# Index queries for fewer token tiles, modulation sums on TensorE and later keys in a hybrid attention, retention and expert block

## The chip, the cores and the metric

The kernel runs on one core of a Trainium2 chip. The metric is the device time of one execution in microseconds (us); the median over several executions is compared. Engines are named as in the profile: PE is TensorE, DVE is VectorE, ACT is ScalarE, POOL is GpSimd, and SP is the engine that mostly issues DMAs. PEld is TensorE loading a stationary operand.

## The reference, cut to what matters

One transformer-like layer over 1024 tokens of width 1024. Only the beginning matters for the change:

```
mod = c @ w_ada + b_ada;  sh1, sc1, gt1, sh2, sc2, gt2 = split(mod, 6)      # 6 x 1024
h   = rmsnorm(x, g) * (1 + sc1) + sh1                                       # 1024 tokens x 1024
qa, ka, va, qi, ki, wi, qb, kb, vb, gb = split(h @ w_in)                     # 4688 columns
# sparse attention, by blocks of 128 queries; qi has 16 index heads of 64, ki one, wi 16 weights
score = sum_h wi[h] * relu(qi[h] . ki / 8)      # causal by chunks of 64 keys
sel   = top_k(score, 256)                       # softmax attention over the selected keys only
```

Then come retention on the second group of heads, the output projection, a mixture of 32 experts (top 2 in one group of 8) and a last norm. A query of token tiles 0 and 1 (tokens 0 to 255) sees at most 256 keys, so its top 256 are all of them; its scores decide nothing.

## The kernel before, in words

Tokens are worked in 8 tiles of 128. There are 5 instruction streams, ordered by hand, with semaphores between them. The part that the change touches runs up to the first score.

**Loads (SP, L467 to L488).** SP issues in order: the whole table of constants (`cst`, 1190 columns), four small vectors, the 8 tiles of x, the 80 columns of w_in for key and index weights (`w_keys`), the columns sc1 and then sh1 of w_ada (4 MB each, in five DMAs, L481), and the first 512 columns of w_in (`load_weights(0)`, L475). After the transposes of x it issues the second 512 columns, and when both index chunks are projected (`a_proj` at `FIRST[RETAIN]`) the third.

**Norm and turn.** ACT squares x (L752), POOL takes the root (L645), DVE scales the tiles (L1045), PE transposes them (L1658), ACT copies the result to `hT` (L764).

**Modulation sums.** DVE multiplies w_ada by c row block by row block and adds (L1054, L1056: 16 instructions of 128x1024, each waited for). This leaves 128 partial sums for each column. PE adds them over the partitions with 8 products against a column of ones for each of the two parts (L1672), which also puts the result in columns. DVE adds the bias (L1060 to L1064) and applies scale and shift to `hT` (L1069, 16 instructions of 128x512; the first half of the tokens first).

**Keys.** PE computes 80 columns (64 of the index key, 16 weights) in plain fp32, over all tokens (L1708, 16 matmuls), ahead of any projection. ACT copies them out (L809, L813), PE turns them (L1716), DVE rotates them (L1135 to L1144), PE turns them again (L1722), and DVE writes `kiD` (L1147).

**Projections in three passes.** Every other projection splits both operands in a rounded high part and a rest: ACT makes the high part (`split_high` L783, `hidden_high` L790), DVE the low part (`split_low` L1118, `hidden_low` L1127), and PE adds high x high, high x low and low x high (`split_product`, L1651 to L1653). A unit is one tile of tokens by one chunk of columns: `project(u)`, 8 steps of 3 matmuls of 128x512. The index queries are chunks 0 and 1, with 8 units each. For each unit ACT copies the result (L805), DVE rotates 8 heads (L1080 to L1086), PE turns the tile (`a_turn`, L1684), and DVE writes `qiT` (L1100). `a_copy` of the first three units waits for the turned keys (`key_pe` at 5).

**Beside it.** ACT issues 8 DMAs that clear `y_dram` (L772, 3 MB each), one after every second copied unit. POOL loads the later modulation columns in 8 steps of 2 MB (L651): the first when 8 units are projected, each further one when PE has used the one before (`late_used`, L1737). `late_products` holds the PE stream while it waits for its load.

**Scores.** For tiles 2 to 7 and 16 heads, 96 units: PE (L1752), relu on ACT (L830), weighted sum on DVE (L1167, L1169). One step of `late_products` stands after every 12 units, the first after 7. PE starts the scores when all turned units are in `qiT`.

The rest (retention projections, top-k by bisection, attention, experts) is not edited but for numbering: units are looked up in a list `UNIT` where `divmod(u, T)` stood.

Of the kernel before, what the change touches and what calls it, by code (L numbers as in the profile page):

```python
# [6 lines left out]
F32 = mybir.dt.float32  # L7
# [9 lines left out]
P = 128  # L17
# [41 lines left out]
FIRST_SCORED = TOPK // P  # L59
SCORED = range(FIRST_SCORED, T)  # L60
# [6 lines left out]
def constant_table():  # L67
# [4 lines left out]
    parts["before"] = (p[:, None] < p[None, :])  # L72
    parts["causal"] = (p[None, :] >= p[:, None])
# [3 lines left out]
    lg = np.log1p(-np.exp2(-5.0 - np.arange(HB)))  # L77
    parts["kfac"] = np.exp(-(p[:, None] + 1.0) * lg[None]) * HD ** -0.5
# [42 lines left out]
def block_kernel(nc, x, ccol, pos, w_ada, b_cols, b_gt1, b_sc2, b_sh2, b_gt2, g_cols, g_ffn, g_final, w_in, w_o, w_router,  # L121
                 w_up, w_gate, w_down, const, out):
    ctx = ExitStack()
    with ctx:
# [22 lines left out]
        def sb_before(name, shape):  # L147
# [16 lines left out]
        ada_slot = [BIG[:, 8192:16384].rearrange("p (k c) -> p k c", k=KD),  # L164
                    BIG[:, 16384:24576].rearrange("p (k c) -> p k c", k=KD)]
# [67 lines left out]
        W0 = work([("sq", (D,)), ("mac", (2, D)), ("ang", (T, 40)), ("k", (T, 40)), ("r", (T, 40)), ("c", (T, 40))])  # L233
        WA = work([("tmp", (3, 512)), ("s1", (128,)), ("s2", (128,)), ("trq", (2, 512)), ("R", (3, 1024))])
        w_keys = WK[:, 4352:4992].rearrange("p (k c) -> p k c", k=KD)
        keys_turned = WK[:, 0:1024]
        keys = WK[:, 1024:1664].rearrange("p (t c) -> p t c", t=T)
        key_rows = WK[:, 1664:2688].rearrange("p (t c) -> p t c", t=T)
        key_s1, key_s2 = [WK[:, a:a + 128].rearrange("p (t a d) -> p t a d", t=T, a=2) for a in (2688, 4992)]
# [89 lines left out]
        UNITS = len(CHUNKS) * T  # L329
        FIRST = {c: c * T for c in (INDEX, RETAIN, ATTEND)}  # L330
        turned = [u for u in range(UNITS) if CHUNKS[u // T][0] not in ("qb", "kb", "vb", "gb", "va")]
        NTURN = len(turned)
        TURN1 = RETAIN * T
        copied = [u for u in range(UNITS) if not RETAIN * T <= u < ATTEND * T]
        NCOPY = len(copied)

        def evacuated(u):

            c, t = divmod(u, T)
# [22 lines left out]

        ADA_PARTS = (((0, 4),), ((4, 8),), ((0, 4),), ((4, 6), (6, 8)))

        def ada_landed(part, a):

            return G("ada_last") if a == 6 else G(f"slot{part}")
# [97 lines left out]
        def _(sp):  # L465

            for dst, src in ((cst[:, :], const), (cc[:, :], ccol), (bc[:, :, :], b_cols), (gc[:, :], g_cols),  # L467
                             (posi[:, :], pos)):
                sp.dma_start(dst, src).then_inc(G("ld_const"), 16)
# [23 lines left out]
            for n in range(RETAIN, ATTEND):  # L493
                if n > RETAIN:
                    sp.wait_ge(G("a_proj"), T * n)
# [13 lines left out]
            sp.wait_ge(G("a_proj"), T * ATTEND)  # L509
# [12 lines left out]
            for step in range(3 * T):  # L522
# [108 lines left out]
            for s in range(NF):  # L631
                sp.wait_ge(G(f"slot{s}"), 16 + 16 * (T // NF))
# [3 lines left out]
        def _(pool):  # L636
# [16 lines left out]

            for m in range(2 * T):
# [91 lines left out]
        def _(act):  # L746
# [30 lines left out]

            def split_high(n, part=None):

                act.wait_ge(G(f"ld_w{n % 3}"), 16 * (n // 3 + 1))  # L780
                raw_, _, hi = W[n]
# [3 lines left out]
            def hidden_high(half):  # L785

                part = slice(512 * half, 512 * half + 512)
                for k in range(KD):
                    act.wait_ge(G("hT_ready"), KD * half + k + 1)
                    own.go(A(hT_hi[:, k, part], hT[:, k, part], ACT.Copy), G("hT_hi"))  # L790

            def a_copy(u):
                name, _, w = CHUNKS[u // T]
                t = u % T
# [3 lines left out]
                else:  # L798
# [3 lines left out]
                    else:  # L802
                        act.wait_ge(G("key_pe"), 5)
# [3 lines left out]
            hidden_high(0)  # L807
            act.wait_ge(G("key_pe"), 1)
            own.go(A(keys_turned[0:KEYS, 0:512], PS[0:KEYS, 6, :], ACT.Copy), G("key_act"))  # L809
            split_high(0)  # L810
            hidden_high(1)
            act.wait_ge(G("key_pe"), 2)
            own.go(A(keys_turned[0:KEYS, 512:1024], PS[0:KEYS, 7, :], ACT.Copy), G("key_act"))  # L813
            act.wait_ge(G("key_pe"), 3)
            own.go(A(keys.rearrange("p (b t) c -> p b t c", b=2),
                     PS[:, 6:8, 0:4 * KEYS].rearrange("p b (t c) -> p b t c", t=4), ACT.Copy), G("key_act"))
# [47 lines left out]
            for u in range(FIRST[RETAIN], FIRST[ATTEND]):  # L864
                n, t = divmod(u, T)
# [156 lines left out]
        def _(dve):  # L1022
# [25 lines left out]
            for n in range(2 * KD):  # L1048
                s, k = divmod(n, KD)
                mac = W0["mac"][:, s]  # L1050
# [1028 lines left out]
```

## Time and profile before

| | |
|---|---|
| runs | 1634.56, 1636.85, 1636.9 us; median 1636.85 |
| profiled execution | span 1634.3 us from first to last instruction; no time of its own is listed, and the lowest run is 0.3 us over the span |
| mean granted PE clock | 0.944 of full |
| instructions | 21594 |
| moved by DMA | 368 MB, mean 225 GB/s |

The profile is of one execution. "Busy" counts an engine's instructions, idle time is what stands before them, and the releaser is what ended that idle time. PEclk is the share of the full TensorE clock that was granted: 1.00 is 2.4 GHz, 0.50 is 1.2 GHz.

### The profile page before, as it was taken

What the parts mean: (1) busy time and instruction counts of PE and PEld (TensorE: products, weight loads), DVE (VectorE), ACT (ScalarE), POOL (GpSimd) and SP (SyncE); (2) the same over time, 40 slices, a digit from 0 to 9 for tenths busy, and PEclk for the clock granted to TensorE, in tenths of its full rate; (3) what the DMA queues carried; (4) which work ended last, traced back from release to release, by engine and by line L of the source; (5) the groups of instructions that cost most, each with busy time, mean ns of one, the idle gap of its engine ahead of it and who ended that gap; (6) DMA issues with size and microseconds to landing.
All of it is one profiled execution on the core that took longest, in us unless ns stands there. A gap on an engine that the chain in (4) does not pass through costs nothing.

```text
span 1634.3 us, 21594 instructions
## 1 busy us (share of the span) xinstructions
PE 1460.1 (89%) x7420; PEld 1137.3 (70%) x7420; DVE 1125.2 (69%) x1513; ACT 908.6 (56%) x1224; POOL 268.6 (16%) x191
## 2 busy tenths in 40 slices
PE   3899899999999899788899965999999999999980
PEld 2588445888887787455666654788888888888860
DVE  6732798672247994433344455999999999999967
ACT  5321577878995111323444422777777777777742
POOL 0000110240001000200000001233223223223215
PEclk9899999999999989589999986999999999999995
DMA  9198643213233233311111116999999999999987
GB/s 368 67 330 315 229 155 110 100 66 111 99 117 133 66 129 129 126 52 65 65 52 53 46 52 244 358 394 399 404 401 401 395 397 398 394 404 395 393 325 268
DMA packets 102566, 368.01 MB, mean 225 GB/s; under 512 B 11232, under 2 KB 23648, under 8 KB 77792
## 3 DMA queue, kind: packets, MB, share of 16 engines
q1 hardware_dynamic: 74208, 291.58, 46.8%
q10 hardware_dynamic: 17024, 41.95, 6.7%
q0 software_dynamic: 11264, 33.57, 5.7%
q8 instruction: 42, 0.69, 0.2%
q14 instruction: 28, 0.23, 0.0%
HBM read 306.24 MB, written 69.21 MB: 230 GB/s over the span
## 4 chain that ended last, share of the span: by engine, by line
PE 73%; DVE 14%; ACT 4%; issue 4%; DMA 3%; POOL 2%; SPq 0%; DVEq 0%; ACTq 0%; POOLq 0%
PE PS L1651 19%; PE PS L1653 19%; PE PS L1652 19%; PE PS L1752 3%; PE PS L1775 2%; PE PS L1974 2%; PE PS L1862 2%; PE PS L1849 2%; DMA WK<-in_w_ada 1%; DVE WK L1056 1%; DVE wlo L1497 1%; PE PS L1708 1%; PE PS L1949 1%; DVE ACC L1169 1%; PE PS L1992 1%
## 5 line engine op out<-in xcount | busy, mean ns | idle before, releaser
L1497 DVE TENSOR_TENSOR wlo<-raw,whi 128x2048 fp32r<-128x2048 f32 x192 | 436.3, 2287 | 39.7 <-ACT whi L963 38.0
L963 ACT ACTIVATE whi<-raw 128x2048 fp32r<-128x2048 f32 x192 | 364.0, 1913 | 126.7 <-DVE WK L1580 80.8
L1651 PE MATMUL PS<-whi,xhi 128*128 128x512 f32 x512 | 204.0, 398 | 4.4 <-DVE xlo L1567 3.2
L1653 PE MATMUL PS<-whi,xlo 128*128 128x512 f32 x512 | 201.3, 393 | 0.0
L1652 PE MATMUL PS<-wlo,xhi 128*128 128x512 f32 x512 | 200.3, 391 | 0.0
L845 ACT ACTIVATE KV<-ACC,WK 128x1024 int8<-128x1024 f32 (+4 forms) x160 | 147.5, 926 | 23.7 <-DVE WK L1192 21.1
L1651 PE MATMUL PS<-KVR,BIGR 128*128 128x512 f32 x320 | 126.9, 396 | 1.1 <-ACT WK L830 1.1
L1653 PE MATMUL PS<-KVR,BIGR 128*128 128x512 f32 x320 | 124.9, 390 | 0.0
L1652 PE MATMUL PS<-KVR,BIGR 128*128 128x512 f32 x320 | 124.5, 389 | 0.0
L696 POOL COPY wcol<-tw 128x1 f32 (+1 forms) x32 | 63.0, 1968 | 371.5 <-DVE WK L1601 371.5
L1651 PEld LDWEIGHTS PS<-whi,xhi 128*128 128x128 f32 x512 | 97.2, 190 | 24.7 <-DVE xlo L1567 4.0
L1653 PEld LDWEIGHTS PS<-whi,xlo 128*128 128x128 f32 x512 | 96.7, 189 | 21.0
L1652 PEld LDWEIGHTS PS<-wlo,xhi 128*128 128x128 f32 x512 | 96.8, 189 | 19.3
L1651 PE MATMUL PS<-whi,hhi 128*128 128x512 f32 x256 | 104.3, 407 | 2.7 <-DVE hlo L1572 2.7
L1653 PE MATMUL PS<-whi,hlo 128*128 128x512 f32 x256 | 101.1, 395 | 0.0
L1652 PE MATMUL PS<-wlo,hhi 128*128 128x512 f32 x256 | 100.8, 394 | 0.0
L805 ACT ACTIVATE WK<-PS 128x512 f32<-128x512 f32 x32 | 18.9, 596 | 137.6 <-PE PS L1684 64.7
L1169 DVE SCALAR_TENSOR_TENSOR ACC<-WK,wsc,ACC 128x384 f32<-128x384 f32 (+5 forms) x90 | 85.6, 952 | 10.8 <-ACT WK L830 8.0
L830 ACT ACTIVATE WK<-PS 128x384 f32<-128x384 f32 (+5 forms) x96 | 70.0, 757 | 35.3 <-PE PS L1752 24.4
L1752 PE MATMUL PS<-KV,BIG 64*128 64x512 f32 (+3 forms) x320 | 86.1, 552 | 1.9 <-ACT WK L830 0.9
L920 ACT ACTIVATE WK<-PS 128x512 f32<-128x512 f32 (+3 forms) x48 | 23.7, 541 | 107.2 <-PE PS L1849 107.1
L1476 DVE TENSOR_TENSOR WK<-PS,KV 128x512 f32<-128x512 f32 x16 | 11.1, 692 | 96.2 <-PE PS L1653 96.2
(328 smaller groups left out, 2907.0 us busy)
## 6 DMA issues: line engine op xcount, KB each, us to landing
raw<-in_w_gate SPq DMA_DIRECT2D x64, 1024.0 KB, 7.7
raw<-in_w_up SPq DMA_DIRECT2D x64, 1024.0 KB, 7.6
raw<-in_w_down SPq DMA_DIRECT2D x64, 1024.0 KB, 7.0
y_dram<-zero ACTq DMA_DIRECT2D x8, 3072.0 KB, 11.3
WK<-in_w_ada POOLq DMA_DIRECT2D x16, 1024.0 KB, 7.5
y_dram<-WK ACTq DMA_DIRECT2D x32, 512.0 KB, 6.5
KV<-in_w_in SPq DMA_DIRECT2D x5, 2048.0 KB, 9.4
KV<-in_x SPq DMA_DIRECT2D x16, 512.0 KB, 5.3
```

The costliest lines, as they stand in the source:

```text
L696: nc.gpsimd.tensor_copy(wcol[:, s:s + 1], column).then_inc(G("m_w"), 1)
L830: own.go(A(WA["R"][:, u % 3, 0:K], PS[:, b:b + 2, :].rearrange("p b c -> p (b c)")[:, 0:K], ACT.Relu), G("sc_relu"))
L845: own.go(A(signs[i], ACC[:, ACC_OFF[i]:ACC_OFF[i] + K], ACT.Sign, bias=sel_try.bitcast(F32)[:, col:col + 1], accum_out=sel_count[:, col:co ...
L963: nc.scalar.activation(whi[:, slot], raw[:, q], ACT.Copy).then_inc(G("m_hi"), 1)
L1169: own(V.scalar_tensor_tensor(acc, R, wsc[:, i, h:h + 1], acc, ALU.mult, ALU.add), G("sc_acc"))
L1497: V.tensor_tensor(wlo[:, slot], raw[:, q], whi[:, slot].bitcast(F32), ALU.subtract)\
L1651: mm(out_, x_hi, w_hi, start=first, stop=False)
L1652: mm(out_, x_hi, w_lo, start=False, stop=False)
L1653: return mm(out_, x_lo, w_hi, start=False, stop=final)
L1752: last = mm(PS[:, 2 * (u % 3) + b, 0:w], qiT[rows, h // 2, tile(i)], kiD[rows, 512 * b:512 * b + w], start=True, stop=True)
L1775: last = mm(PS[:, 2 * (h % 2) + b, 0:w], queries(i)[rows, h // 2, :], kaT[rows, h // 2, 512 * b:512 * b + w], start=True, stop=True)
L1849: last = tr(PS[:, 4 + n % 2, P * (b % 4):P * (b % 4) + P], WC["S"][:, (HA * i + h) % 3, P * b:P * b + P], ident)
```

## The change

Index queries are projected only for tiles 4, 5, 6, 7, 2, 3 of chunk 0 and 2 to 7 of chunk 1: 12 units for 16. The modulation sums go to PE, four column groups of 32 beside each other. Hidden state and weights of chunk 0 are made ready in four pieces, the second half of the tokens first, and PE works the first four units together, step by step of k. Keys become two products in three passes, after four and after six units. Of the constants only the first 168 columns are loaded first; `w_keys` and the other constants come behind the weights. The clearing DMAs are issued after each of the first 8 units.

```diff
+HALVES = (1, 0)
-        ada_slot = [...]
+        ada_both = BIG[:, 8192:24576].rearrange("p (a k c) -> p a k c", a=2, k=KD)
+        IN_ORDER = {0: (4, 5, 6, 7, 2, 3), 1: tuple(SCORED)}
+        UNIT = [(c, t) for c in range(len(CHUNKS)) for t in IN_ORDER.get(c, range(T))]
+        FIRST = [[c for c, _ in UNIT].index(c) for c in range(len(CHUNKS))]
+        TURN1 = FIRST[RETAIN]
...
 SP
-            for dst, src in ((cst[:, :], const), (cc[:, :], ccol), (bc[:, :, :], b_cols), (gc[:, :], g_cols),
+            for dst, src in ((cst[:, 0:early], const[:, 0:early]), (cc[:, :], ccol), (bc[:, :, :], b_cols),
...
-            sp.dma_start(w_keys, win_v[:, :, KEYS_AT:KEYS_AT + KEYS]).then_inc(G("ld_k0"), 16)
-            for s, part in enumerate((1, 0)):
-                for h in range(2):
-                    for a, b in ADA_PARTS[2 * s + h]:
-                        sp.dma_start(ada_slot[s][:, a:b], wada_v[:, part, a:b]).then_inc(ada_landed(2 * s + h, a), 16)
-            load_weights(0)
+            for k in range(KD):
+                sp.dma_start(ada_both[:, :, k], wada_v[:, 0:2, k]).then_inc(G(f"slot{k // 2}"), 16)
+            _, c0, w = CHUNKS[0]
+            sp.dma_start(W[0][0][:, 0:4], win_v[:, 0:4, c0:c0 + w]).then_inc(G("ld_w0"), 16)
+            sp.dma_start(W[0][0][:, 4:8], win_v[:, 4:8, c0:c0 + w]).then_inc(G("ld_first"), 16)
+            sp.dma_start(w_keys, win_v[:, :, KEYS_AT:KEYS_AT + KEYS]).then_inc(G("ld_k0"), 16)
+            sp.dma_start(cst[:, early:], const[:, early:]).then_inc(G("ld_rest"), 16)
 POOL
-                pool.wait_ge(*((G("late_used"), n) if n else (G("a_proj"), T)))
+                pool.wait_ge(*((G("late_used"), n) if n else (G("a_proj"), FIRST[1])))
 ACT
+            act.wait_ge(G("mod_sum"), 1)
+            own.go(A(W0["row"], PS[:, 0, :], ACT.Copy), G("mod_row"))
...
-                    else:
-                        act.wait_ge(G("key_pe"), 5)
...
+            for part in range(4):
+                split_high(0, part)
+                hidden_high(0, (2 * part, 2 * part + 1))
+            act.wait_ge(G("ld_k0"), 16)
+            own.go(A(w_keys_hi, w_keys, ACT.Copy), G("key_hi"))
+            hidden_high(1, range(KD))
+            split_high(1)
...
             for u in range(TURN1):
                 a_copy(u)
-                if u == 3:
-                    split_high(1)
-                if u % 2 == 0:
-                    zero_rows(u // 2)
+                if u in (2, 5):
+                    keys_copy(u // 3)
+                if u == 6:
+                    (copy of the turned keys)
+                if u < 8:
+                    zero_rows(u)
 DVE
-            for n in range(2 * KD):
-                (the 16 multiply-adds of 128x1024, and the bias of the first part)
             dve.wait_ge(G("hT_raw"), T)
-            dve.wait_ge(G("pe_cols"), 2)
-            own(V.tensor_tensor(mod[:, 1, :], PS[:, 1, 0:KD], bc[:, 1, :], ALU.add))
+            dve.wait_ge(G("pe_cols"), 1)
+            own.go(V.tensor_tensor(halves(mod[:, 1, :]), PS[:, 0:2, 0:4], halves(bc[:, 1, :]), ALU.add))
+            own(V.tensor_tensor(halves(mod[:, 0, :]), PS[:, 2:4, 0:4], halves(bc[:, 0, :]), ALU.add))
+            own(V.scalar_tensor_tensor(mod[:, 0, :], mod[:, 0, :], 1.0, gc[:, :], ALU.add, ALU.mult))
...
-            hidden_low(0)
-            split_low(0)
-            hidden_low(1)
+            for part in range(4):
+                ks = (2 * part, 2 * part + 1)
+                hidden(0, ks)
+                split_low(0, part)
+                hidden_low(0, ks)
+            dve.wait_ge(G("key_hi"), 1)
+            own.go(V.tensor_tensor(w_keys_lo, w_keys, w_keys_hi.bitcast(F32), ALU.subtract), G("key_lo"))
+            hidden(1, range(KD))
+            hidden_low(1, range(KD))
+            split_low(1)
...
                 a_rotate(m)
                 if m >= 1:
                     a_evacuate(m - 1)
-                if m == 4:
-                    split_low(1)
+                if m == 5:
+                    rotate_keys()
+                if m == 8:
+                    (the two copies to kiD)
 PE
-            for s in range(2):
-                pe.wait_ge(G("mac_done"), s + 1)
-                for k in range(KD):
-                    last = mm(PS[:, s, k:k + 1], W0["mac"][:, s, P * k:P * k + P], ones[:, 0:1], start=True, stop=True)
+            for k in range(KD):
+                if k % 2 == 0:
+                    pe.wait_ge(G(f"slot{k // 2}"), 32)
+                for g in range(4):
+                    last = mm(PS[32 * g:32 * g + 32, 0, :], cc[:, k:k + 1].to_broadcast([P, 32]),
+                              ada_both[:, g // 2, k, 512 * (g % 2):512 * (g % 2) + 512], start=(k == 0), stop=(k == KD - 1))
+            last.then_inc(G("mod_sum"), 1)
+            pe.wait_ge(G("mod_row"), 1)
+            for g in range(4):
+                for b in range(4):
+                    rows = slice(32 * g, 32 * g + 32)
+                    last = mm(PS[:, g, b:b + 1], W0["row"][rows, P * b:P * b + P], ident[rows, 32 * g:32 * g + 1],
+                              start=True, stop=True)
+            last.then_inc(G("pe_cols"), 1)
...
+            def keys_of(at):
+                (waits for key_lo and for all of hT_lo of that half)
+                for k in range(KD):
+                    last = split_product(out_, w_keys_hi[:, k], w_keys_lo[:, k], hT_hi[:, k, part], hT_lo[:, k, part],
+                                         k == 0, k == KD - 1)
...
+            for k in range(KD):
+                pe.wait_ge(G("hT_lo"), k + 1)
+                if k % 2 == 0:
+                    pe.wait_ge(G("w_lo"), k // 2 + 1)
+                for u in range(4):
+                    last = split_product(PS[:, bank_of(u), :], ... k == 0, k == KD - 1)
+            keys_of(0)
+            for u in range(4, TURN1):
                 project(u)
+                if u == 4:
+                    a_turn(0)
+                a_turn(u - 3)
+                if u == 5:
+                    keys_of(1)
                 (turns of the keys after units 6 and 8, where 0 and 2 stood)
```

## Rows read from the trace of the kernel before

**Rows 1.** The page, busy time (us, share of the span, instructions) of each engine.
```profile
PE 1460.1 (89%) x7420; PEld 1137.3 (70%) x7420; DVE 1125.2 (69%) x1513; ACT 908.6 (56%) x1224; POOL 268.6 (16%) x191
```
**Rows 2.** Timeline, 30 to 70 us: start, us, engine, line, operation, output<-inputs.
```profile
30.78 1.06 PE L1658 MATMUL PS<-cst,KV 128*128 128x128 f32 x8 [0.29 <-ACT BIG L764]
...
41.01 5.25 DVE L1056 SCALAR_TENSOR_TENSOR WK<-BIG,cc,WK 128x1024 f32<-128x1024 f32 x4
...
46.32 3.57 PE L1672 MATMUL PS<-ones,WK 128*128 128x1 f32 x16 [6.86 <-DVE WK L1056]
50.02 0.17 DVE L1064 TENSOR_TENSOR mod<-PS,bc 128x8 f32<-128x8 f32 x1 [3.76 <-PE PS L1672]
50.23 7.40 DVE L1069 TENSOR_SCALAR BIG<-BIG,mod 128x512 f32<-128x512 f32 x16
...
50.92 16.25 PE L1708 MATMUL PS<-BIG,WK 128*80 128x512 f32 x32 [1.03 <-DVE BIG L1069]
...
60.39 4.91 DVE L1127 TENSOR_TENSOR BIGR<-BIG,BIGR 128x512 fp32r<-128x512 f32 x8 [2.77 <-issue]
...
65.21 4.62 DVE L1118 TENSOR_TENSOR WKR<-WK,ACCR 128x1024 fp32r<-128x1024 f32 x4
```
**Rows 3.** The loads of w_ada: all five, and the issue under way at 22.7 us with its landing time.
```profile
L481 SPq DMA_DIRECT2D BIG<-in_w_ada x5: 1122/2548/5025, 8.0 to 20.3; - x5
...
BIG<-in_w_ada SPq DMA_DIRECT2D x1, 1024.0 KB, 18.6
```
**Rows 4.** Timeline, 66 to 170 us, PE and ACT.
```profile
66.60 0.79 PE L1651 MATMUL PS<-ACCR,BIGR 128*128 128x512 f32 x1
...
72.54 0.72 PE L1716 MATMUL PS<-cst,WK 80*128 80x80 f32 x8
...
84.23 1.03 PE L1722 MATMUL PS<-cst,WK 128*128 128x128 f32 x8
...
90.65 0.60 PE L1684 MATMUL PS<-cst,WK 128*128 128x128 f32 x4
...
156.76 0.60 ACT L805 ACTIVATE WK<-PS 128x512 f32<-128x512 f32 x1 [5.30 <-PE PS L1684]
...
161.97 1.03 PE L1684 MATMUL PS<-cst,WK 128*128 128x128 f32 x8
...
167.27 4.91 PE L1752 MATMUL PS<-KV,BIG 64*128 64x384 f32 x14 [0.88 <-DVE BIG L1100]
```
**Rows 5.** Busy time by stretch: us, PE, PEld, DVE, ACT, POOL busy, PEclk, DMA share, GB/s.
```profile
4.00:6.00 2.00, 0.00 (x0) 0.00 (x0) 0.46 (x2) 0.00 (x0) 0.00 (x0) 1.00 0.96 209
...
22.00:30.00 8.00, 7.38 (x52) 6.84 (x51) 7.89 (x10) 5.30 (x6) 0.00 (x0) 1.00 1.02 409
...
36.00:46.00 10.00, 3.46 (x16) 3.37 (x16) 9.68 (x10) 0.00 (x0) 0.00 (x0) 0.50 1.04 387
...
55.00:55.50 0.50, 0.50 (x2) 0.26 (x1) 0.50 (x2) 0.13 (x1) 0.00 (x0) 0.50 0.00 0
55.50:56.00 0.50, 0.50 (x2) 0.15 (x1) 0.50 (x2) 0.00 (x0) 0.00 (x0) 0.92 0.00 0
```
**Rows 6.** Late modulation loads (landing us min/median/max), and PE's first step on them.
```profile
DMA to landing us min/median/max: 5.6/7.5/12.3
...
172.12 1.92 PE L1737 MATMUL PS<-WK,cc 128*32 128x512 f32 x16
...
174.37 1.43 POOL L651 DMA_DIRECT2D WK<-in_w_ada  x2 [57.15 <-PE PS L1737]
```
**Rows 7.** Clearing DMAs on ACT's queue, and DMA traffic in two stretches (columns as rows 5).
```profile
85.38 0.45 ACTq L772 DMA_DIRECT2D y_dram<-zero  x1
...
86.03 1.55 ACTq L772 DMA_DIRECT2D y_dram<-zero  x1
...
96.00:100.00 4.00, 4.00 (x21) 3.30 (x20) 1.45 (x5) 0.60 (x1) 0.00 (x0) 1.00 1.03 372
...
172.00:176.00 4.00, 4.00 (x26) 1.55 (x26) 2.01 (x4) 1.76 (x5) 1.43 (x2) 1.00 0.20 36
```

More of the change, by code:

```diff
@@ L77, in constant_table @@
     lg = np.log1p(-np.exp2(-5.0 - np.arange(HB)))
+    parts["before"] = (p[:, None] < p[None, :])
+    parts["causal"] = (p[None, :] >= p[:, None])
     parts["kfac"] = np.exp(-(p[:, None] + 1.0) * lg[None]) * HD ** -0.5
@@ L231, in work @@
             return out_
-        W0 = work([("sq", (D,)), ("mac", (2, D)), ("ang", (T, 40)), ("k", (T, 40)), ("r", (T, 40)), ("c", (T, 40))])
+        W0 = work([("sq", (D,)), ("row", (512,)), ("gap", (1536,)), ("ang", (T, 40)), ("k", (T, 40)), ("r", (T, 40)), ("c", (T, 40))])
         WA = work([("tmp", (3, 512)), ("s1", (128,)), ("s2", (128,)), ("trq", (2, 512)), ("R", (3, 1024))])
         w_keys = WK[:, 4352:4992].rearrange("p (k c) -> p k c", k=KD)
[L236 to L239, printed above, removed]
+        w_keys_lo, w_keys_hi = [WKR[:, a:a + 640].rearrange("p (k c) -> p k c", k=KD) for a in (4352, 4992)]
+        keys_turned = WK[:, 1792:2816]
+        keys = WK[:, 2816:3456].rearrange("p (t c) -> p t c", t=T)
+        key_rows = WK[:, 1792:2816].rearrange("p (t c) -> p t c", t=T)
+        key_s1, key_s2 = [WK[:, a:a + 128].rearrange("p (t a d) -> p t a d", t=T, a=2) for a in (5632, 5760)]
         W = {}
@@ L1119, in split_low, with hidden_low @@
                            G("w_lo"))
[L1121 to L1126 removed]
+            def hidden_low(at, ks):
+                part = slice(512 * HALVES[at], 512 * HALVES[at] + 512)
+                for k in ks:
+                    dve.wait_ge(G("hT_hi"), KD * at + k + 1)
                     own.go(V.tensor_tensor(hT_lo[:, k, part], hT[:, k, part], hT_hi[:, k, part].bitcast(F32),
@@ L1137, in _ @@
-            own.go(V.tensor_tensor(key_s2[:, :, 0], pairs[:, :, 1], nsinT[:, :, 0:8], ALU.mult))
-            own.go(V.tensor_tensor(key_s2[:, :, 1], pairs[:, :, 0], sinT[:, :, 0:8], ALU.mult))
-            own.go(V.tensor_copy(key_rows[:, :, 0:64], keys[:, :, 0:64]))
-            own.go(V.tensor_copy(key_rows[:, :, 64:128], keys[:, :, 0:64]))
-            own.wait()
-            for half in range(2):
-                rows = key_rows[:, :, 64 * half:64 * half + 16].rearrange("p t (a d) -> p t a d", a=2)
-                own.go(V.tensor_tensor(rows, key_s1, key_s2, ALU.add), G("key_dve") if half else None)
@@ L1145, in _ @@
-            for half in range(2):
-                dve.wait_ge(G("key_pe"), half + 4)
-                own.go(V.tensor_copy(kiD[:, 512 * half:512 * half + 512], PS[:, 6 + half, :]), G("key_dve"))
+            for part in range(4):
[5 more added lines that the diff above has]
+            own.go(V.tensor_tensor(w_keys_lo, w_keys, w_keys_hi.bitcast(F32), ALU.subtract), G("key_lo"))
@@ new lines, in _, with rotate_keys @@
+            hidden(1, range(KD))
+            hidden_low(1, range(KD))
+            split_low(1)
+            pairs = keys[:, :, 0:16].rearrange("p t (a d) -> p t a d", a=2)
+            def rotate_keys():
+                dve.wait_ge(G("key_act"), 3)
+                own.go(V.tensor_scalar(wsc[:, :, :], keys[:, :, 64:80], NIH ** -0.5 * HD ** -0.5, None, ALU.mult))
+                own.go(V.tensor_tensor(key_s1, pairs, cosT[:, :, 0:8].unsqueeze(2).to_broadcast([P, T, 2, 8]), ALU.mult))
+                own.go(V.tensor_tensor(key_s2[:, :, 0], pairs[:, :, 1], nsinT[:, :, 0:8], ALU.mult))
+                own.go(V.tensor_tensor(key_s2[:, :, 1], pairs[:, :, 0], sinT[:, :, 0:8], ALU.mult))
+                own.go(V.tensor_copy(key_rows[:, :, 0:64], keys[:, :, 0:64]))
+                own.go(V.tensor_copy(key_rows[:, :, 64:128], keys[:, :, 0:64]))
+                own.wait()
+                for half in range(2):
+                    rows = key_rows[:, :, 64 * half:64 * half + 16].rearrange("p t (a d) -> p t a d", a=2)
+                    own.go(V.tensor_tensor(rows, key_s1, key_s2, ALU.add), G("key_dve") if half else None)
```

135 lines of the change are left out of this document (56 added, 79 removed).

## The prediction

> **What bounds the kernel now.** The page comes first: PE is busy for 89% of the span, DVE for 69% [rows 1], and the chain that ended last is mostly PE. That is an average, so the timeline of the edited part comes next. It shows three stretches up to the first score at 167.27 us. (1) Up to 50.23 us PE mostly waits. DVE scales x and then makes 16 multiply-adds of 1.3 us; its last four stand at 41.01 to 46.26 [rows 2]. The last load of w_ada was issued at 20.3 us and took 18.6 us [rows 3], so it was there at 38.9. DVE, not the load, ends this stretch. (2) From 50.23 to 66.60 us PE works on keys in plain fp32, 16.25 us, and no projection can start [rows 2]. (3) From 66.60 us PE runs unit after unit. ACT's copy of a unit takes 0.60 us and stands idle for 5.30 before it, so a unit takes 5.9; four transposes are 0.6 of that [rows 4], so 24 matmuls take 5.3. Nothing else delays it: PE is the bound, and each unit taken out is worth all of its time. Behind 167 us there is nothing that starts at a fixed time, so what is won by then is kept, but for the late loads (below).
>
> **The start, up to the scaled hidden state (now 50.23 us).** The first load shrinks from 595 to 84 KB. The queue moves 209 GB/s in 4 to 6 us and 409 later [rows 5], so 0.52 MB is 1.3 to 2.5 us; I take 1.7. The squares, the root and the scaling follow x, so the last transposes end at 31.84 - 1.7 = 30.1 us [rows 2]. Ahead of the last of w_ada there are now 0.85 MB less (constants and `w_keys`), 2.1 us at 409 GB/s: landed at 36.8. PE's sums are 32 matmuls of the form that the late steps have, 8 matmuls in 1.92 us [rows 6], so 0.96 us for each k and 7.7 in all. Six k can be done by 35.9; the last two wait for their load and end at 36.8 + 1.9 = 38.7. Then, new and in series: ACT's copy of 128x512, 0.60 [rows 4] and some 0.3 to hand over; 16 small fp32 matmuls. In rows 2 eight such matmuls (16 records) took 3.57 us, 0.223 a record, at a granted clock of 0.50 [rows 5]. Eight transposes with the same 128 columns of weights at clock 1.00 took 1.06, 0.13 each [rows 2]. Bounds for 32 records are therefore 4.2 and 7.1 us; I take 4.2 less pipelining, 3.6, since PE has been busy without a break. Two adds and one multiply, 0.2 each, 0.7 with the hand-over. Sum: 38.7 + 0.9 + 3.6 + 0.7 = 43.9. **Saved here: 6.3 us** (2.8 with the dear columns). Of DVE 16 instructions go; nobody else waited for them. SP issues 8 + 2 + 2 DMAs for 7, at about 0.4 each where it isn't held by the queue; the weights of chunk 0 land after w_ada by 1 MB each 2.6 us, at 39.4 and 42, before DVE wants them.
>
> **From there to the first projection.** DVE makes two scaled pieces (7.40/16 = 0.46 each), one low part of weights (4.62/4 = 1.16) and a first low part of the hidden state (4.91/8 = 0.61) [rows 2]: 2.7, with hand-over 2.9 us. ACT's pieces fit beside these. Before, it was 16.4 us.
>
> **PE from there to the first score.**
> - First four units together: 4 x 5.3 = 21.2. DVE needs 3.3 us for two k (0.93 + 1.16 + 1.23) and PE 5.3, so PE isn't starved. Clock: PE has then been idle for some 3.5 us. Before, with PE's last transpose at 31.84, the clock was 0.50 from 36 us on, and after work began at 50.92 it stayed at 0.50 until 55.5 [rows 2, 5]. So I add half of 4.7 us, 2.4. Bounds: 0 if the clock doesn't fall, 3. The keys took this loss before, so it only moves.
> - Keys: 2 x 24 matmuls of 512 columns, priced as a unit: 10.6 us for 16.25. In three passes rather than fp32 they are cheaper, and off the start.
> - Eight more units: 42.4, with the 0.1 us each that a period shows over its parts 43.2. Eight transposes sets ahead of the tail: 4.8. Turns of the keys 0.72 + 1.03 = 1.75 [rows 4], as before.
> - Tail from the last matmul of a unit to the first score: 167.27 - 161.97 = 5.3 [rows 4], unchanged.
>
> Sum 2.9 + 21.2 + 2.4 + 10.6 + 43.2 + 4.8 + 1.75 + 5.3 = 92.2 us, where it was 167.27 - 50.23 = 117.0. **Saved: 24.8 us.** Four units and their turns are 23.6 of it; keys 16.25 to 10.6 and their DVE work beside PE make the rest, and the clock's 2.4 comes off. The first score stands at 43.9 + 92.2 = 136.1 us, 31.2 earlier.
>
> **Waits that are added.** ACT's first copies no longer wait for the turned keys. DVE's `rotate_keys` waits for ACT's copy of the turned keys; behind it are rotations that PE wants a unit later (5.3 us), so it is covered. PE waits after unit 8 for the rotation, which has had a whole unit. I price these at nothing; their cover is one unit of PE, and if one failed it would cost 1 to 2 us.
>
> **Clearing DMAs and late loads.** The clearing starts at about 71 us, for 85.4. It is 25.2 MB, 68 us at 372 GB/s [rows 7]; with the first late load (5.5) and the third chunk's weights (5.5) the queue is busy until 71 + 1.5 + 79 = 151 us. The second late load is issued 7.1 us after the first score (174.37 - 167.27 [rows 4, 6]), at 143 us, for 8 us beside that traffic. In the kernel before the traffic had just ended (36 GB/s in 172 to 176 [rows 7]). In traffic such a load took 12.3 us where the median is 7.5 [rows 6], and PE holds the scores for it. Bounds: 0 and 4.8, once. I take **2 us lost**. Later late loads find the queue free, as now.
>
> **Sum.** 6.3 + 24.8 - 2 = 29.1 us off a span of 1634.3, 1605.2. The median of the runs lies 2.5 over the span, so the forecast is 1607.7, rounded to 1608.
>
> **Rivals.**
> (A) ACT's stream is held by its own clearing DMAs. The second one, issued right behind the first, took 1.55 us for 0.45 [rows 7]; now three to eight follow each other closely. If each held ACT until an earlier one had drained (3.15 MB, 8.4 us), ACT's copies would be stretched to 8 steps of 8.4 us from 71 us. Up to unit 8 PE, with four units' lead and the keys between, needs them no sooner; the last turns would wait up to 138 us where I have PE at 130: 8 us lost, 1616. For it: the 1.55. Against: no third in close order is shown. Chance 0.08.
> (B) PE's clock is low when the sums begin. The transposes just ahead took 0.13 us each and the granted clock was 1.00 in 22 to 30 us, when PE did nothing but these [rows 2, 5], so work of this kind seems to have kept it. But 1.00 is also shown while PE had done nothing yet, so the rows don't prove it. If the sums (7.7) and the columns (3.6) ran at half, the last pair would land behind PE: 30.1 + 15.4 + 0.9 + 7.1 + 0.7 = 54.2, not 43.9: 10.3 us lost, 1618. Chance 0.05. The Trainium skill ("TensorE: Matmul & The Clock Gate", Part 4) has a rule for this side: it says that the full clock doesn't engage for transposes, which don't count as PE being busy. The trace here speaks against it so far, by the 1.00 and the 0.13 us.
> (C) The slower side: PE never gets its clock up in the index stage, because the first four units come in pieces on which it waits, and each wait lets the clock fall. Then 12 units and the keys, 74.2 us at full clock, would take 148: 74 lost against 31 won, 1682. It decides from 31 us of matmul work at half clock on. Against: DVE's 3.3 us for a piece for which PE needs 5.3 at full clock and 10.6 at half; before, the clock rose 4.7 us after work began and stayed [rows 5]. Chance 0.02.
> (D) The late loads hurt twice: the second and the third each at 12.3 us, and the dear columns too: 2.8 + 24.8 - 9.6 = 18.0, 1619. Chance 0.04.
> (E) The units are left out in name only, with PE waiting elsewhere in the same stretch (a load of chunk 1, a bank): no change. Against: chunk 1 is loaded at the same byte count as now and wanted at 60 us. Chance 0.01.
>
> **How the numbers follow.** The forecast's own case has 0.80. Its terms: columns 0 to +3.5, clock -2.4 to +0.6, late load -2 to +2.8, covers 0 to +2, x earlier by 0.4 less or 0.8 more. That is 1602 to 1615. A and part of B lie up to 1617. Range 1602 to 1617. About 0.2% (3.3 us) is what a measurement of this kernel can tell from no change. Faster 0.97, same 0.01, slower 0.02.
>
> **What would show it.** Right: L1056 is gone; 64 records of column-group matmuls end near 38.7 us; first L1651 near 47; first L1752 near 136; the keys as 48 matmuls of 80x512 at 0.22 us each in the three lines of the three passes; 12 copies L805, the later ones 5.9 us apart. Wrong: sums that end after 45 us, a gap of PE over 1 us between 70 and 130 us, ACT's copies behind a long ACT queue row, L1737 waiting over 4 us for its load, or a span after the first score that differs from 1467 us by more than 4.

## The result and the profile after

The changed kernel took 1608.91 us (median of 4 runs, 1607.99 to 1613.12) where the kernel before took 1636.7: a ratio of 0.9831, 95% interval 0.9813 to 0.9849, or 27.8 us less. The forecast was 1608.0. The profiled execution has a span of 1605.9 us (forecast 1605.2). The total is right to 1 us, but partly by luck, since two errors cancel in it: the first score stands at 139.50 us where 136.1 was forecast, and what follows it took 1466.4 us, 0.6 less than before (1634.3 - 167.27 = 1467.0) where 2 more were forecast. A second trace of the same kernel, `after_again` below, has a span of 1603.5 us and its first score at 137.94, so the errors themselves are only known to 1 or 2 us.

The page of the changed kernel, busy time of each engine; it answers to [rows 1]:

```profile
PE 1433.7 (89%) x7388; PEld 1117.5 (70%) x7388; DVE 1099.5 (68%) x1478; ACT 907.6 (57%) x1222; POOL 268.0 (17%) x191
```

PE's busy time fell by 26.4 us and the span by 28.4, so most of the gain is matmul work that is gone. This is a net over the whole span and doesn't name the parts: at the start 5.5 us are won from a chain of DVE for which PE waited, while PE was busy there for 19.2 us where it had been 16.7. The timeline of the start (start, us, engine, line, operation, output<-inputs) answers to [rows 2]:

```profile
30.59 1.06 PE L1672 MATMUL PS<-cst,KV 128*128 128x128 f32 x8 [0.29 <-ACT BIG L764]
31.58 5.36 PE L1687 MATMUL PS<-BIG,cc 128*32 128x512 f32 x48
...
38.93 1.92 PE L1687 MATMUL PS<-BIG,cc 128*32 128x512 f32 x16 [2.00 <-DMA BIG<-in_w_ada]
...
40.98 0.60 ACT L779 ACTIVATE WK<-PS 128x512 f32<-128x512 f32 x1 [8.27 <-PE PS L1687]
...
41.63 2.47 PE L1694 MATMUL PS<-cst,WK 32*128 32x1 f32 x32 [0.78 <-ACT WK L779]
...
44.68 1.00 DVE L1072 TENSOR_SCALAR BIG<-BIG,mod 128x512 f32<-128x512 f32 x2
...
47.48 0.80 PE L1665 MATMUL PS<-ACCR,BIGR 128*128 128x512 f32 x1 [3.38 <-DVE BIGR L1129]
48.07 0.63 PE L1666 MATMUL PS<-WKR,BIGR 128*128 128x512 f32 x1
```

The sums on PE are done for six k at 36.9 us and then wait 2.0 us for the last piece of w_ada. Scaling starts at 44.68 us for 50.23, and the first projection at 47.48 for 66.60: 19.1 us earlier. The granted clock over this stretch (us, busy time of PE, PEld, DVE, ACT and POOL, then PEclk, DMA share, GB/s), as in [rows 5]:

```profile
36.00:40.00 4.00, 2.00 (x24) 0.45 (x20) 0.00 (x0) 0.00 (x0) 0.00 (x0) 1.00 1.04 388
40.00:44.00 4.00, 3.22 (x40) 2.37 (x32) 0.00 (x0) 1.65 (x2) 0.00 (x0) 1.00 1.10 347
44.00:46.00 2.00, 0.10 (x1) 0.01 (x1) 1.72 (x6) 0.74 (x2) 0.00 (x0) 0.80 1.05 382
...
51.00:52.00 1.00, 1.00 (x4) 0.76 (x3) 1.00 (x3) 0.23 (x1) 0.00 (x0) 0.50 0.05 18
52.00:54.00 2.00, 2.00 (x10) 1.65 (x9) 2.00 (x4) 1.88 (x3) 0.00 (x0) 1.00 0.01 4
```

The sums and the columns ran at 1.00 (2.4 GHz); while PE then waited for DVE the clock fell to 0.50, and it came back at 52 us. The middle and the tail, timeline of ACT's queue, ACT and PE, answering to [rows 4] and [rows 7]:

```profile
72.23 0.60 ACT L808 ACTIVATE WK<-PS 128x512 f32<-128x512 f32 x1 [0.97 <-PE PS L1667]
...
83.69 4.69 ACTq L772 DMA_DIRECT2D y_dram<-zero  x1
...
88.50 13.41 ACTq L772 DMA_DIRECT2D y_dram<-zero  x1
102.00 0.60 ACT L808 ACTIVATE WK<-PS 128x512 f32<-128x512 f32 x1 [12.93 <-PE PS L1707]
102.05 8.17 ACTq L772 DMA_DIRECT2D y_dram<-zero  x1
...
103.14 0.77 PE L1759 MATMUL PS<-cst,WK 80*128 80x80 f32 x8 [1.70 <-ACT WK L822]
...
133.75 1.03 PE L1707 MATMUL PS<-cst,WK 128*128 128x128 f32 x8
137.52 1.11 PE L1707 MATMUL PS<-cst,WK 128*128 128x128 f32 x4 [0.86 <-DVE WK L1089]
139.50 5.43 PE L1793 MATMUL PS<-KV,BIG 64*128 64x384 f32 x14 [0.87 <-DVE BIG L1103]
...
147.12 1.43 POOL L650 DMA_DIRECT2D WK<-in_w_ada  x2 [55.22 <-PE PS L1778]
...
155.59 1.92 PE L1778 MATMUL PS<-WK,cc 128*32 128x512 f32 x16 [1.68 <-DMA WK<-in_w_ada]
```

The fifth clearing DMA held ACT's queue for 13.41 us (the first late load, 2 MB, was issued meanwhile, at 90.2 us); the copy that PE needs for the turn of the keys stood behind it, and PE waited 1.70 us.

### The profile page after: what moved, and what is told of

It is laid out like the page before. It is cut to its first block, busy times and chain, and to the rows that moved or that the text cites. A ratio compares the mean times of both kernels' runs of the same rounds, so it can differ in the third digit from the quotient of the medians.

```text
span 1605.9 us, 21481 instructions
## 1 busy us (share of the span) xinstructions
PE 1433.7 (89%) x7388; PEld 1117.5 (70%) x7388; DVE 1099.5 (68%) x1478; ACT 907.6 (57%) x1222; POOL 268.0 (17%) x191
## 4 chain that ended last, share of the span: by engine, by line
PE 73%; DVE 12%; ACT 5%; issue 3%; DMA 3%; POOL 2%; ACTq 1%; SPq 1%; DVEq 0%; POOLq 0%
PE PS L1665 19%; PE PS L1667 19%; PE PS L1666 18%; PE PS L1793 4%; PE PS L1816 2%; PE PS L2015 2%; PE PS L1903 2%; PE PS L1890 2%; DMA BIG<-in_w_ada 1%; ACTq L772 1%; DVE wlo L1511 1%; ACT KV L856 1%; PE PS L1990 1%; DVE ACC L1183 1%; PE PS L2033 1%
## 5 line engine op out<-in xcount | busy, mean ns | idle before, releaser
L856 ACT ACTIVATE KV<-ACC,WK 128x1024 int8<-128x1024 f32 (+4 forms) x160 | 147.5, 926 | 23.8 <-DVE WK L1206 21.3
L1665 PE MATMUL PS<-KVR,BIGR 128*128 128x512 f32 x304 | 120.4, 396 | 1.1 <-ACT WK L841 1.1
L1667 PE MATMUL PS<-KVR,BIGR 128*128 128x512 f32 x304 | 118.6, 390 | 0.0
L1666 PE MATMUL PS<-KVR,BIGR 128*128 128x512 f32 x304 | 118.3, 389 | 0.0
L931 ACT ACTIVATE WK<-PS 128x512 f32<-128x512 f32 (+3 forms) x48 | 23.5, 541 | 107.8 <-PE PS L1890 107.8
```

The lines of the kernel that those rows point to most:

```text
L856: own.go(A(signs[i], ACC[:, ACC_OFF[i]:ACC_OFF[i] + K], ACT.Sign, bias=sel_try.bitcast(F32)[:, col:col + 1], accum_out=sel_count[:, col:co ...
L1665: mm(out_, x_hi, w_hi, start=first, stop=False)
L1666: mm(out_, x_hi, w_lo, start=False, stop=False)
L1667: return mm(out_, x_lo, w_hi, start=False, stop=final)
```

## The experiments

All are edits of the changed kernel. The table gives, from each timeline, the first projection, the first score and the rest of the span behind it, then the median of the runs and the ratio to the kernel before with its 95% interval. The edits were run in three sets, each beside its own runs of the kernel before: the first four edits (kernel before 1636.7 us), `clear_sp` to `three` (1637.2), and the last four (1638.4). So runs of different sets are compared by their ratios.

| kernel | first projection | first score | rest | median us | ratio |
|---|---|---|---|---|---|
| before | 66.60 | 167.27 | 1467.0 | 1636.7 | 1 |
| changed | 47.48 | 139.50 | 1466.4 | 1608.9 | 0.9831 (0.9813 to 0.9849) |
| units16 | 46.34 | 160.20 | 1469.6 | 1631.9 | 0.9972 (0.9961 to 0.9983) |
| dve_sums | 52.22 | 143.24 | 1466.8 | 1613.0 | 0.9860 (0.9839 to 0.9881) |
| load_order | 51.74 | 143.06 | 1469.4 | 1611.9 | 0.9843 (0.9826 to 0.9859) |
| unit_major | 45.97 | 139.31 | 1467.4 | 1609.7 | 0.9836 (0.9820 to 0.9853) |
| clear_sp | 46.55 | 137.14 | 1465.6 | 1606.3 | 0.9814 (0.9796 to 0.9832) |
| warm | 47.20 | 139.33 | 1470.0 | 1608.4 | 0.9815 (0.9796 to 0.9833) |
| low_first | 45.94 | 136.79 | 1465.8 | 1607.3 | 0.9820 (0.9803 to 0.9837) |
| three | 45.49 | 133.68 | 1469.5 | 1604.3 | 0.9793 (0.9777 to 0.9810) |
| load_bridge | 48.44 | 140.97 | 1469.0 | 1612.2 | 0.9839 (0.9821 to 0.9857) |
| after_again | 46.72 | 137.9 | 1465.6 | 1608.6 | 0.9829 (0.9815 to 0.9843) |
| two | 45.60 | 135.7 | 1466.4 | 1606.0 | 0.9815 (0.9802 to 0.9829) |
| three_again | 45.99 | 133.8 | 1468.2 | 1603.2 | 0.9788 (0.9775 to 0.9802) |

How far may a single trace be trusted? The last piece of w_ada came between 37.4 and 38.9 us in ten traces of kernels that are alike up to there (mean 38.1), and the rest of the span was 1465.6 to 1470.0. So differences of under 2 us are read from a stretch inside the trace, counted from its own start, and not from spans.

**units16: the four units again.**

```diff
-        IN_ORDER = {0: (4, 5, 6, 7, 2, 3), 1: tuple(SCORED)}
+        IN_ORDER = {0: (4, 5, 6, 7, 0, 1, 2, 3)}
```

> The changed kernel with all 16 units of index queries again (tiles 4 to 7, 0 to 3, and 0 to 7); everything else stays. Theory: PE is the bound from the first projection on, so each of the four units costs its whole 5.9 us: first score at 139.5 + 23.6 = 163.1 us, or 161.4 if PE's 1.7 us of waiting for ACT at the turn of the keys goes; span 1628 to 1630. Rival: PE is paced by ACT's held queue in this stretch, and the units were partly covered by it: less than 15 us more.

From the first projection to the first score it took 113.86 us for 92.02: 21.8 more. PE didn't wait at the turn of the keys here (its only wait from 47 to 150 us is the one ahead of the first projection). The turn has the same place in the order of units; what differs is ACT's hold. The first late load is issued when chunk 0 is projected, here at 107.6 us for 90.2, and the fifth clearing DMA, now without it, held ACT's queue for 9.24 us for 13.41. So the four units cost 21.8 + 1.7 = 23.5 us, 5.9 each, as the theory has it. Counted from the turn of the keys alone, behind this wait, it is 59.56 us to the first score for 36.36: 23.2. The runs say 23 us (1631.9 - 1608.9). This one line is five sixths of the whole gain.

**dve_sums: the sums on DVE as before.** The loads of w_ada, the 16 multiply-adds, the two sets of column products and their waits are taken back; the units, keys and the other loads are not.

> The changed kernel with the modulation sums and their loads as they were (16 multiply-adds on DVE, 16 column products on PE); units, keys and the other loads stay changed. Theory: DVE's chain of 16 x 1.31 us ends near 46.2 us and scaling starts near 50 for 44.7: 5.3 us more at the first score and in the span (about 1611). Rival: the loads of w_ada set the start in both, so under 2 us more.

```profile
45.52 3.57 PE L1705 MATMUL PS<-ones,WK 128*128 128x1 f32 x16 [7.10 <-DVE WK L1077]
...
49.43 1.00 DVE L1091 TENSOR_SCALAR BIG<-BIG,mod 128x512 f32<-128x512 f32 x2
```

In its timeline scaling starts at 49.43 us, 4.8 to 5.5 later than in the two traces of the changed kernel (44.68, 43.92); the first score is 3.7 and 5.3 later, and the runs are 4.1 us more, with intervals that overlap. In the traces the theory holds. The rival's part of truth is that the sums on PE end on a load: they can't be made to pay more without that load.

**load_order: constants and key weights first.**

```diff
-            for dst, src in ((cst[:, 0:early], const[:, 0:early]), ...
+            for dst, src in ((cst[:, :], const), ...
+            sp.dma_start(w_keys, ...)          # ahead of w_ada, and no load of the rest
```

> The changed kernel with the whole table of constants loaded first and the key weights ahead of w_ada, as before the change. Theory of the prediction: the sums wait for the last piece of w_ada and 0.85 MB more is ahead of it, so it lands 2.1 us later (41.0 for 38.9) and the first score is 2 us later. Rival, from the trace of the changed kernel, where the last piece landed at 38.9 us just as before the change: the order of these small loads does not set that landing, 0 to 0.5 us.

```profile
39.44 3.64 PE L1684 MATMUL PS<-BIG,cc 128*32 128x512 f32 x16 [3.26 <-DMA BIG<-in_w_ada]
...
48.94 1.00 DVE L1070 TENSOR_SCALAR BIG<-BIG,mod 128x512 f32<-128x512 f32 x2
...
36.00:40.00 4.00, 0.74 (x8) 0.20 (x8) 0.00 (x0) 0.00 (x0) 0.00 (x0) 0.78 1.03 389
40.00:44.00 4.00, 3.22 (x17) 0.54 (x9) 0.00 (x0) 0.80 (x2) 0.00 (x0) 0.50 1.04 386
```

Neither expectation is right. The piece landed at 39.44 us, 0.5 to 2 later than in the ten traces, 1.4 later than their mean, where the theory had 2.1. But scaling started at 48.94, 4.3 us later than in the first trace of the changed kernel. PE had idled 3.26 us for 2.0, the clock fell to 0.50 before the last sums, and these took 3.64 us for 1.92 and the columns 4.50 for 2.47. A small delay of a load was multiplied by the clock: 1.7 us of the loss stand in the last sums and 2.0 in the columns.

**load_bridge: the same, with PE kept busy ahead of the last two k.**

```diff
+                if k == 6:
+                    pe.wait_ge(G("hT_raw"), T - 1)
+                    for _ in range(3):
+                        mm(PS[:, 4, :], ident, zero[:, :], start=True, stop=True)
```

> The kernel with the old order of the small loads, which had scaling start at 48.9 us for 44.7, with three fp32 products on zeros in PE's stream ahead of the last two k of the sums, where PE had idled 3.3 us. Theory: most of that loss was the clock (sums 3.64 us for 1.92, columns 4.50 for 2.47, at 0.50 granted), so it comes back: columns near 2.5 us, scaling starts at 45 to 45.7. Rival: the landing of the last piece alone sets it: scaling starts at 48.5 to 49 again.

```profile
37.12 2.84 PE L1684 MATMUL PS<-zero,cst 128*128 128x512 f32 x6
39.89 1.92 PE L1688 MATMUL PS<-BIG,cc 128*32 128x512 f32 x16
42.59 2.47 PE L1695 MATMUL PS<-cst,WK 32*128 32x1 f32 x32 [0.78 <-ACT WK L777]
...
36.00:40.00 4.00, 4.00 (x22) 1.30 (x18) 0.00 (x0) 0.00 (x0) 0.00 (x0) 1.00 1.03 390
```

The theory holds: the last sums start no earlier (39.89), but they and the columns are back at full clock, and scaling starts at 45.64 us, 3.3 us earlier. The runs don't show it (1612.2 and 1611.9 in two sets): in this trace a part is given back by the first score (92.5 us from the first projection, 91.3 in load_order), with the clock low at the start of the projections. So the small loads' order is worth about 3 us in the runs (1611.9 against 1608.9, with intervals that overlap), most of it by way of the clock.

**unit_major: the first four units one after another.** The loops over k and u are exchanged, with DVE's waits on the first unit only.

> The changed kernel with its first four units one after the other (all 8 k of one unit, then the next) for k by k over four units. Theory: DVE makes one k in 1.65 us where one unit's k takes PE 0.7, so PE waits through the first unit; it ends near 58.8 us and the other three take 16.6: 3.3 us more at the first score. Less if the clock's slow stretch falls into these waits: at least 1 us. Rival: no difference, because DVE's pieces are ahead anyway.

```profile
PE PS L1665 <- DVE BIGR L1129: 3.5, 3, 1.6
```

These are its waits from 47 us on, behind the first projection (45.97): PE waited for DVE three times more, 3.5 us in all, and none of these waits is in the changed kernel. The first matmul of the keys shows where the four units end (changed kernel, then unit_major):

```profile
71.86 0.39 PE L1665 MATMUL PS<-BIGR,WKR 128*80 128x512 f32 x1
...
73.89 0.39 PE L1665 MATMUL PS<-BIGR,WKR 128*80 128x512 f32 x1
```

From the first projection that is 27.92 us for 24.38, and 24.04 in the second trace: 3.5 to 3.9 us more, so the theory of 3.3 holds. The whole stretch to the first score took only 1.3 to 2.1 us more (93.3 us for 92.0 and 91.2), because another effect hides part of it: here the clearing DMAs start at 60.7 us for 70.0, the fifth holds ACT's queue for 3.52 us, and PE's 1.7 us of waiting at the turn of the keys are gone. The piece between the second keys' first matmul and that turn shows it: 11.5 us for 13.4. In the runs the net can't be told from nothing (1609.7).

**clear_sp: clearing issued by SP.**

```diff
+            sp.wait_ge(G("pool_set"), 1)       # behind load_weights(1)
+            for u in range(8):
+                (the same DMA, issued by SP)
-                if u < 8:
-                    zero_rows(u)
```

> The changed kernel with the eight clearing DMAs issued by SP right behind the second chunk's weights, for ACT behind its copies. Theory: ACT's queue is no longer held (12.9 us in one piece before), PE's wait of 1.7 us at the turn of the keys goes, and the traffic ends before the scores: 1.7 us less at the first score, up to 1.7 more less behind it where PE waited for the second late load; span 1602.5 to 1604.2. Rival: the hold costs nothing, or the earlier traffic delays other loads: 0 or slower.

PE's wait at the turn of the keys is gone. The stretch from the first projection took 90.6 us for 92.0 and 91.2. That is a gain of less than 1.7 us, since the first four units took 25.3 us here for 24.4 and 24.0, with the clock at 0.50 for longer (it rose between 52 and 53 us, 6 us behind the first projection). The median is 2.6 us lower, which the interval alone doesn't separate from the changed kernel. Behind the first score nothing clear was won: PE still waited 1.6 us there for late loads, though the clearing was over (4 GB/s in 140 to 144 us). So the clearing isn't what makes these waits.

**warm: three products on zeros before the first projection.**

```diff
             last.then_inc(G("pe_cols"), 1)
+            pe.wait_ge(G("hT_raw"), T - 1)
+            for _ in range(3):
+                mm(PS[:, 4, :], ident, zero[:, :], start=True, stop=True)
```

> The changed kernel with three fp32 products of 128x512 on zeros (their result is not used) between the column products and the first projection, where PE idled 3.4 us. Theory: the granted clock stays at 1.00 and the first 4.5 us of projection work no longer run at 0.50: 2.2 us less at the first score. Rival: the clock falls all the same, or rises later: no gain, at most 0.3 us lost.

```profile
43.76 4.40 PE L1699 MATMUL PS<-zero,cst 128*128 128x512 f32 x6
47.20 1.32 PE L1665 MATMUL PS<-ACCR,BIGR 128*128 128x512 f32 x1
48.35 0.39 PE L1666 MATMUL PS<-WKR,BIGR 128*128 128x512 f32 x1
...
44.00:45.00 1.00, 1.00 (x3) 0.43 (x3) 0.93 (x5) 0.01 (x1) 0.00 (x0) 0.95 1.08 389
45.00:46.00 1.00, 1.00 (x2) 0.33 (x1) 1.00 (x2) 1.00 (x2) 0.00 (x0) 0.50 1.05 387
...
48.00:49.00 1.00, 1.00 (x5) 0.84 (x4) 1.00 (x3) 0.76 (x2) 0.00 (x0) 0.85 0.86 315
...
100.00:102.00 2.00, 0.30 (x4) 0.21 (x4) 1.36 (x5) 1.08 (x2) 0.00 (x0) 1.00 1.01 398
102.00:104.00 2.00, 2.00 (x13) 1.72 (x12) 0.18 (x1) 0.00 (x0) 0.00 (x0) 0.73 1.04 405
104.00:106.00 2.00, 2.00 (x6) 1.51 (x6) 0.00 (x0) 0.00 (x0) 0.00 (x0) 0.50 1.05 410
```

The expected 2.2 us didn't come. The clock fell at about 45 us although PE was at work, while the products on zeros ran; they took 4.40 us for 2.84 in load_bridge and overran. It came back at 48.3, so the matmuls from 48.35 on are at full speed, and the four units took 23.3 us for 24.4 and 24.0: 0.7 to 1.1 us won. But in the same trace the clock fell a second time at 103 us, after PE's 1.7 us of waiting for ACT, which it hadn't done in the changed kernel's traces after the same wait. From the turn of the keys to the first score it took 37.5 us for 36.4 and 35.9, so the win was lost again: 92.1 us for the whole stretch.

**low_first: the first low part made while DVE idles.**

```diff
+            split_low(0, 0)
             dve.wait_ge(G("hT_raw"), T)
             dve.wait_ge(G("pe_cols"), 1)
...
-                split_low(0, part)
+                if part:
+                    split_low(0, part)
```

> The changed kernel with the first low part of the weights made before DVE waits for the columns; DVE idled 18 us there. Theory: the chain from the modulation to the first projection is DVE's, so 1.14 us less from there: first projection at 46.3 for 47.5, and the same at the first score. Rival: ACT's high part of the hidden state becomes the last (0.2 to 0.5 us less only), or nothing.

```profile
43.95 1.00 DVE L1081 TENSOR_SCALAR BIG<-BIG,mod 128x512 f32<-128x512 f32 x2
...
45.94 0.79 PE L1675 MATMUL PS<-ACCR,BIGR 128*128 128x512 f32 x1 [2.57 <-DVE BIGR L1138]
```

From scaling to the first projection it is 1.99 us for 2.80: 0.8 us of the expected 1.14, because ACT's high part, which had been made beside this low part, is now waited for in part. PE idles 2.57 us for 3.38.

**three: the three edits together**, with two products on zeros for three.

> The changed kernel with the three edits together: clearing by SP, PE kept busy (two products on zeros), the first low part made early. Theory: the three gains are in series on the path and add: 4 to 6.5 us less than the changed kernel, span about 1600.5. Rival: they overlap, under 3 us.

**after_again, two and three_again**, run beside each other: the changed kernel unedited, the edits of clear_sp and low_first, and three once more.

> The changed kernel unedited, to have it on one chip with its variants. Ratio to the kernel before as recorded, 0.983 within 0.0015; first score within 1.2 us of 139.5, since the last piece of w_ada landed between 37.4 and 38.9 us in kernels that start alike.

> Clearing by SP and the first low part early, without the products on zeros. Theory: 1.4 and 1.1 us in series at the first score, 2.5 us under the changed kernel, and no dip of the clock in the scores such as the three edits together had (score stage 103.0 to 103.7 us, not 106.5): device time 2.5 to 3.5 us under the changed kernel. Rival: no difference that can be measured.

> The three edits together once more. Theory: first score again near 133.7 us and, if the longer score stage (106.5 us) was an accident of where the clock's steps fell, about 103.5 us there this time, so span near 1600.2. Rival: the score stage is longer each time, since the late loads now come at another moment: 106.5 again.

```profile
42.70 3.67 PE L1713 MATMUL PS<-zero,cst 128*128 128x512 f32 x4
45.49 1.11 PE L1679 MATMUL PS<-ACCR,BIGR 128*128 128x512 f32 x1
46.44 0.39 PE L1680 MATMUL PS<-WKR,BIGR 128*128 128x512 f32 x1
...
133.68 5.33 PE L1810 MATMUL PS<-KV,BIG 64*128 64x384 f32 x14 [0.87 <-DVE BIG L1116]
```

These rows are of three. With all three edits the first score came at 133.7 and 133.8 us in two traces, 4 to 6 us earlier than in the changed kernel (137.9, 139.5), and the stretch from the first projection took 88.2 and 87.8 us for 92.0 and 91.2. In two, without the products on zeros, it takes 90.1, so these bring 1.9 to 2.3 us against that trace. All of it stands in the first four units (22.9 and 22.5 us for 24.8); from the turn of the keys on the three traces agree (35.9 us). Against low_first, whose four units took 23.7 us, it is 0.8 to 1.2, as in warm, so the size of this gain is open.

Some is given back: from the first score to the first projection behind the scores it took 107.6 and 107.0 us, for 104.8 and 104.2 in the changed kernel and 104.0 in two. Against the changed kernel this is 2.8 us both times, which refuses the accident and speaks for the rival. It goes with the clock: in the 10 us from the first score the mean granted clock was 0.66 and 0.50, for 0.77 and 0.83 in the changed kernel and 0.83 in two. The first late products show it, in three_again and in two:

```profile
139.81 3.64 PE L1795 MATMUL PS<-WK,cc 128*32 128x512 f32 x16
...
140.47 1.92 PE L1792 MATMUL PS<-WK,cc 128*32 128x512 f32 x16
```

Why the clock is lower there is open.

Against what was expected: three has a span of 1603.2 us where 1600.5 was expected, and its runs are 4.6 us under the changed kernel's, by ratios of 0.9793 and 0.9831. The ratio of after_again came as expected, its first score 1.6 us from 139.5 where 1.2 was allowed. Two is 2.6 us under the changed kernel in the runs and 2.2 at the first score, near the theory's 2.5.

The measured order on one chip is 1608.6, 1606.0, 1603.2 us. The interval of two overlaps that of the changed kernel (ratios 0.9815 and 0.9829), so its gain isn't shown by the runs. That of three_again is apart from it: 0.9788, interval 0.9775 to 0.9802, against 0.9829, 0.9815 to 0.9843. That version beats both kernels.

## Why the prediction was right, point by point

**The units.** "Four units and their turns are 23.6 of it": 23.2 to 23.5 by units16. PE was the bound, as read from its chain and its unbroken stream. No run takes back the keys in three passes, so what they bring is not shown by itself. From scaling to the first score the traces have 117.0 us before and 94.8 after, 22.2 less, and 23.0 less in the second trace: apart from the four units, what changed there brought nothing in sum.

**The start.** The sum had scaling at 43.9 us; it was 44.68 and, in the second trace, 43.92. Its terms were off in both directions. The last piece of w_ada was forecast for 36.8 us and came at 37.4 to 38.9: to take 0.85 MB off ahead of it at 409 GB/s didn't bring 2.1 us. The column products were priced at 3.6 us and took 2.47: 32 records of 32 rows cost 0.08 each, less than the nearest row (0.13 for a transpose) that bounded them. The step "I take 1.7" for an earlier x also failed: the last transposes began at 30.59 for 30.78.

**The first projection** was forecast 2.9 us behind scaling; it was 2.80.

**From there to the first score** 89.3 us were forecast and 92.0 measured. The first four units took from 47.48 to 71.86, 24.4 us for 23.6: the unit price of 5.3 had been read from ACT's idle time, in which the transposes overlap the next matmuls, and the matmuls themselves stand 0.23 us apart (24 make 5.5). The clock's loss was 2.3 us (0.50 until 52.0) for 2.4. The step "I price these at nothing; their cover is one unit of PE" failed at one of the added waits: PE stood 1.70 us at the turn of the keys. With that, two of the prediction's own signs of being wrong came, a gap of PE over 1 us between 70 and 130 us, and ACT's copies behind a long row of its queue, though the forecast of the total held. Its cause is rival A's, at a fifth of its price, and not where A put it: the copy of the second keys stands behind the fifth clearing DMA, well ahead of the last turns. Clear_sp shows it, since the wait goes with the DMAs. That the hold lasted 13.41 us has a second cause by units16, the late load issued in it. The tail was 5.75 us for 5.3, with the last transposes at half clock (1.11 us for 0.66). These three are 0.8, 1.7 and 0.45 us of the 2.7; the other terms cancel but for 0.2.

**The late loads.** 2 us were forecast as lost; the rest of the span was 0.6 us shorter than before. The second late load was issued at 147.12, where 143 was forecast, and the traffic it was to meet ended just then, where 151 was forecast: 409 GB/s in 144 to 146 us, 115 in 147 to 147.5, and 12 in the half us after it. PE waited for it for 1.68 us, about as long as in the kernel before, whose row is this:

```profile
182.66 1.92 PE L1737 MATMUL PS<-WK,cc 128*32 128x512 f32 x16 [1.50 <-DMA WK<-in_w_ada]
```

It was there 8.5 us after its issue for 8.3 before, not the 12.3 that the prediction had taken as its bound. In the second trace it was issued at 145.03, about 1 us before the traffic ended, and the wait was 1.45 us. This is the term that had the wrong size: it hid 2.6 of the 3.4 us that the first score was late. That the total came out to 1 us is luck to that extent.

**The range.** The terms listed for the forecast's own case add up to 1602.5 to 1617 us, not to the 1602 to 1615 that stands there. The stated range of 1602 to 1617 covers them.

**The rivals.** B is refused: the sums followed the transposes at a granted clock of 1.00, two k in 1.92 us. The Trainium skill's sentence that transposes don't count as PE being busy ("TensorE: Matmul & The Clock Gate", Part 4) would have had them at half; the trace decides against it here. But its price was real: load_order shows sums and columns at 0.50 and 3.8 us lost by it, from a cause that B didn't name, PE's wait for a load. C and E didn't come: clock 1.00 from 52 us on, and the units' work gone. D came neither by its late loads nor by its columns.

## What to carry to other kernels

Where an engine runs without a break, work left out is worth its full busy time, and a price taken from what stands between its rows is safer than one from another engine's idle time. Look at what else a queue carries before many DMAs are issued in close order by an engine that also feeds the bound: the issue itself can hold that engine, and a queue with nothing else to do is a better place. A short wait of PE for a load costs more than its length if the granted clock falls in it, as it did in load_order, so the last load before a chain of small products deserves to be early or to be bridged. And two effects in one stretch can hide each other, as in unit_major: cut the stretch at a point between them before you read a price from its length.

## What was not expected of the hardware

- Issuing a DMA took 0.45 us with ACT's queue empty, 4.69 us for the fourth of eight 3 MB transfers, 13.41 for the fifth and about 8 for each further one. The Trainium skill ("DMA: Bandwidth & Descriptors", Issuing engines are not separate DMA queues) calls the sequencer's time for it usually small beside the transfer; here it was as long as the transfer, once several were under way (8.17 us, where 3.15 MB take 8.2 us at the 385 GB/s of 90 to 110 us). With the late load issued later (units16) the fifth took 9.24, the seventh and eighth 9.92 and 11.88.
- PE was shown busy from 41.36 us on in warm, first with the column products and then with those on zeros, and the clock nevertheless fell at about 45 us. In three_again, with the same column products and two of those on zeros, it stayed at 1.00 from 40 to 50 us. In three, the same kernel, it fell just before 43 us, with PE at the column products. What sets the moment is open.
- After a wait of 1.5 to 1.7 us at the same point the clock fell in one trace (warm, to 0.50 at 103 us) and not in six others. A single trace doesn't give the price of such a wait.
